# Delta-rule matmuls on unnormalised keys and queries, with the norms folded into row scalars

## The chip, the cores and the metric

The kernel runs on one core of a Trainium2 chip. The metric is the device time of one execution in microseconds (us). Engines are named as in the profile: PE is TensorE (matmuls; PEld its weight loads), DVE is VectorE, ACT is ScalarE, POOL is GpSimd, SP is the queue that issues the DMAs.

## The reference

One layer over x of shape (1, 1024, 1024) in float32: a mixer and a gated feed-forward block. The change concerns the mixer's head group A, a gated delta rule with 4 heads of 128 by 128. Its core, per head and per chunk of the sequence, is:

```
q, k = l2_normalize(q), l2_normalize(k)            # x * rsqrt(sum(x*x) + 1e-6), per token
L    = strict_lower((beta * k) @ k.T * decay)      # decay[i,j] = exp(gcum_i - gcum_j)
sol  = solve(I + L, [beta * v, beta * k * exp(gcum)])      # u, w
v_new = u - w @ state
o     = (q * exp(gcum)) @ state + lower(q @ k.T * decay) @ v_new
state = state * g_last + (k * exp(gcum_last - gcum)).T @ v_new
```

After it come a per-head RMS norm times a gate, an output projection together with head group B (attention in a sliding window), a residual, and the feed-forward block.

## The kernel before, in words

Three blocks follow each other: project_block (input projection and convolution; it leaves q, k, v per tile in DRAM with channels on the partitions), mix_block (both head groups, output projection, the residual and a norm), ffn_block. The change is in mix_block alone, in the profile about 281 to 713 us.

mix_block works on 8 tiles of 128 tokens. Every engine runs a list of small functions that is written out by hand: a preamble for tile 0, then step(t) for t = 0 to 7. In step t the functions named b_ advance the recurrence of tile t, those named a_ prepare head group A of tile t+1 (the flag a; absent in step 7), c_ are head group B of tile t+1, d_ the output projection of tile t-1 (flag d, from step 1) and the residual and norm of tile t-2 (flag e, from step 2). a_norms and a_square already belong to tile t+2 (flag n, absent from step 6 on). An engine does its list strictly in order; after(engine, counter, tile, k) makes it wait until a counter has reached its k-th event of that tile. PSUM banks have such counters too: full["a1"] counts the fills of a bank, free["a1"] the reads that release it, and fill(name, t, k) makes PE wait for the read k-1.

What matters here, in PE's order within a step: b_ks (keys times state), a_tr (k and v of the next tile to token order, in banks a0 and a1), b_vnew, a_sums (cumulated decays by column; it refills bank a1 and so waits for a_bv), d_tr, c_trq, b_o1 (queries times state), a_trk, b_ds (state update), c_trk, b_o2, a_kk, c_scores, a_kq, the output projection d_mm in pieces, a_trl, and then six levels of a_off and a_inv that build the inverse.

The norms before: a_square squares q and k of tile t+2 in the loaded block on ACT; a_norms sums over channels on PE with a column of ones; a_n2 adds 1e-6 on DVE; a_rnorm takes the power -0.5 on POOL, at the end of step t. a_khat on DVE then makes the unit keys k_tok from bank a0, a_trk and a_kt bring them to channel order in k_t, a_q copies the queries to q_t, a_kout on POOL scales k_tok to k_out, a_beta on POOL makes the mask beta * strict.

The loaded block qkv has one buffer, the left half of a stage; load_qkv waits until its readers are done.

## Time and profile before

| | |
|---|---|
| device time, median of 3 runs | 1465.1 us (1460.33 to 1465.41) |
| the profiled execution | 1462.3 us, of which the span is 1460.5 |
| instructions | 18291 |
| mix stage, first instruction to the first weights of ffn_block | 281 to 713 us |
| step 4 (b_ks of tile 4 to b_ks of tile 5) | 527.74 to 575.93, 48.2 us |
| mean granted clock of PE | 0.965 |

The span goes from the first to the last instruction. Times in the profile count from the start of the span. A granted clock of 1 is 2.4 GHz, of 0.5 is 1.2 GHz. Matmuls in float32 leave two records each, transposes and fp32r matmuls one. Records on PE overlap, so starts tell more than durations there.

### The profile page before, as it was taken

Reading aid. Unit: us, or ns where it says so; the run is one execution under the profiler, and the core shown is the slowest. Engines: PE = TensorE matmul, PEld = TensorE weight load, DVE = VectorE, ACT = ScalarE, POOL = GpSimd, SP = SyncE. Lnnn points to the kernel's source line nnn. Section 1 sums busy time; section 2 is a strip of 40 time slices with the busy share of each in tenths; the row PEclk is TensorE's granted clock in tenths of the full one; section 3 lists DMA queues with packets and bytes.
Section 4 is the critical chain, followed back from the end, with each engine's and each line's share of the span. In section 5 each row is a group of like instructions: output and inputs, shape, how many; then the busy total and the mean of one; then the engine's idle time right before and its main releaser. Section 6 shows DMA issues by size and latency. Waiting matters only on the chain.

```text
span 1460.5 us, 18291 instructions
## 1 busy us (share of the span) xinstructions
PE 1355.5 (93%) x6919; PEld 1145.0 (78%) x6919; DVE 720.7 (49%) x989; ACT 407.7 (28%) x672; POOL 198.9 (14%) x202
## 2 busy tenths in 40 slices
...
DMA packets 63707, 99.39 MB, mean 68 GB/s; under 512 B 4111, under 2 KB 48815, under 8 KB 63663
## 3 DMA queue, kind: packets, MB, share of 16 engines
...
## 4 chain that ended last, share of the span: by engine, by line
PE 48%; POOL 1%; DVE 1%; issue 1%; ACT 0%; POOLq 0%
PE f_ps_up L2038 11%; PE f_ps_up L2039 11%; PE f_ps_up L2040 11%; PE sums L2057 5%; PE sums L2058 5%; PE sums L2056 5%; POOL stage L1765 1%; POOL f_conv L1765 0%; DVE split L1963 0%; POOL f_stat L2022 0%; DVE f_w_lo L1904 0%; ACT f_w_hi L1836 0%; POOLq L1672 0%; DVE f_conv L1976 0%; DVE h_t L1956 0%
## 5 line engine op out<-in xcount | busy, mean ns | idle before, releaser
L2038 PE MATMUL f_ps_up<-split,f_w_hi 128*128 128x512 f32 x704 | 275.7, 392 | 2.2 <-DVE split L1963 2.2
L2039 PE MATMUL f_ps_up<-split,f_w_hi 128*128 128x512 f32 x704 | 275.3, 391 | 0.0
L2040 PE MATMUL f_ps_up<-split,f_w_lo 128*128 128x512 f32 x704 | 275.2, 391 | 0.0
L1909 DVE SCALAR_TENSOR_TENSOR f_conv<-f_ps_up,f_taps,f_conv 128x1023 f32<-128x1023 f32 x88 | 112.8, 1282 | 275.2 <-ACT f_conv L1840 269.7
L2038 PEld LDWEIGHTS f_ps_up<-split,f_w_hi 128*128 128x128 f32 x704 | 133.0, 189 | 30.8 <-DVE split L1963 2.0
L2040 PEld LDWEIGHTS f_ps_up<-split,f_w_lo 128*128 128x128 f32 x704 | 133.0, 189 | 27.8
L2039 PEld LDWEIGHTS f_ps_up<-split,f_w_hi 128*128 128x128 f32 x704 | 133.0, 189 | 27.5
L1840 ACT ACTIVATE f_conv<-f_ps_up,f_taps 128x1024 f32<-128x1024 f32 x44 | 53.2, 1209 | 325.9 <-PE f_ps_up L2040 325.9
L1921 DVE TENSOR_TENSOR h_t<-sums,h_t 128x512 f32<-128x512 f32 x176 | 116.3, 687 | 37.3 <-PE sums L2058 37.1
L2056 PE MATMUL sums<-f_w_hi,f_y_hi 128*128 128x512 f32 x320 | 124.5, 389 | 0.0
L2057 PE MATMUL sums<-f_w_lo,f_y_hi 128*128 128x512 f32 x320 | 124.5, 389 | 0.0
L2058 PE MATMUL sums<-f_w_hi,f_y_lo 128*128 128x512 f32 x320 | 124.5, 389 | 0.0
L2022 POOL TENSOR_TENSOR f_stat<-f_stat,f_power 128x1 f32<-128x1 f32 x8 | 5.4, 671 | 695.4 <-DVE f_stat L2006 695.4
L1904 DVE TENSOR_TENSOR f_w_lo<-stage,f_w_hi 128x2048 fp32r<-128x2048 f32 x33 | 75.6, 2290 | 49.0 <-ACT f_w_hi L1836 49.0
L474 PE MATMUL ps_g<-wbuf,tile_hi 128*128 128x512 f32 (+1 forms) x192 | 69.9, 364 | 6.4 <-DVE wbuf L409 6.4
L1429 PE MATMUL m_ps_a<-m_inv,m_low_t 128*128 128x128 f32 x384 | 57.5, 296 | 19.3 <-DVE m_inv L1148 17.0
L494 PE MATMUL ps_g<-h_hi,wbuf 128*128 128x512 f32 x192 | 74.8, 390 | 0.0
L496 PE MATMUL ps_g<-h_hi,wbuf 128*128 128x512 f32 x192 | 74.7, 389 | 0.0
L495 PE MATMUL ps_g<-h_lo,wbuf 128*128 128x512 f32 x192 | 74.7, 389 | 0.0
L1429 PEld LDWEIGHTS m_ps_a<-m_inv,m_low_t 128*128 128x128 f32 x384 | 50.7, 202 | 29.3 <-DVE m_inv L1148 25.4
L2056 PEld LDWEIGHTS sums<-f_w_hi,f_y_hi 128*128 128x128 f32 x320 | 60.1, 188 | 12.5
L2058 PEld LDWEIGHTS sums<-f_w_hi,f_y_lo 128*128 128x128 f32 x320 | 60.1, 188 | 12.5
...
## 6 DMA issues: line engine op xcount, KB each, us to landing
...
```

What stands on the lines that cost most here:

```text
L494: pe.matmul(bank, w_hi, h_hi[:, k, cols], start=(k == 0), stop=False)
L495: pe.matmul(bank, w_hi, h_lo[:, k, cols], start=False, stop=False)
L1429: op = pe.matmul(bank("a0")[:, h], low_t[:, h], inv[:, h], start=True, stop=True)
L1904: dve.tensor_tensor(w_lo[:, kind], raw[:, slot], w_hi[:, kind].bitcast(F32), ALU.subtract).then_inc(s_wlo, 1)
L1909: op = dve.scalar_tensor_tensor(conv[:, q, k:S], ps_up[:, q % 2, 0:S - k], taps[:, bass.ds(ct + (FTAPS - 1 - k) * 2 * FT, 1)], conv[:, q, ...
L1921: dve.tensor_tensor(cols, ps_dn[:, (2 * t + half) % 4], cols, ALU.add).then_inc(s_acc, 1)
L2038: pe.matmul(bank, hi, h_hi[:, k, cols], start=(k == 0), stop=False)
L2039: pe.matmul(bank, hi, h_lo[:, k, cols], start=False, stop=False)
L2040: op = pe.matmul(bank, lo, h_hi[:, k, cols], start=False, stop=(k == KD - 1))
L2056: pe.matmul(bank, y_of(0, last)[:, k, y], dn_w(0, kind)[:, k, cols], start=(k == 0), stop=False)
L2057: pe.matmul(bank, y_of(0, last)[:, k, y], dn_w(1, kind)[:, k, cols], start=False, stop=False)
L2058: op = pe.matmul(bank, y_of(1, last)[:, k, y], dn_w(0, kind)[:, k, cols], start=False, stop=(k == 1))
```

## The change

Keys and queries are no longer normalised before the matmuls. PE reads them straight from the loaded block, and the norms come in as one scalar per token and head:

- a_khat, a_trk, a_kt and a_q go, with k_tok, k_t and q_t. a_kk, a_kq, b_ks and b_o1 read qkv[par]. The block has two buffers, and load_qkv has other conditions.
- a_square and a_norms do the queries alone. The squares of the keys are summed by ACT (a_ksq) from bank a0, after a_tr of the same step and, in ACT's list, behind b_v_new. a_kn2 on DVE adds 1e-6.
- a_rnorm on POOL moves from the end of a step (for tile t+2) to the head of the next (for the same tile, then t+1). It makes the reciprocal key norm rn, then beta * rn, beta * rn * rn, and beta * rn * rn * I_NEG (I_NEG no longer holds beta), then the reciprocal query norm.
- a_bv scales by beta * rn; a_low takes beta * rn * rn by head in four instructions; b_resid takes the negative one. a_beta goes, and a_masks uses strict alone.
- a_kout moves from POOL to DVE, behind b_state, and reads bank a0; its read releases the bank for a_kk.

The diff, cut to its core (twelve leading blanks removed; the calls of the preamble, which follow the same order, and lines that only pass par on are left out):

```diff
@@ -578,12 +579,12 @@
 a_exp = sb("a_exp", [P, H])
 power = sb("power", [P, 2 * H])
-squares = sb("squares", [P, 2 * H, P])
+squares = sb("squares", [P, H, P])
+k_junk = sb("k_junk", [P, H, P], BF16)
 g_tri = sb("g_tri", [P, H, P])
 norm2 = sb("norm2", [P, 2, 2, 2 * H])
-k_tok = sb("k_tok", [P, H, P])
-k_t = sb("k_t", [P, H, P])
-q_t = sb("q_t", [P, H, P])
+k_gate = sb("k_gate", [P, 2, 3, H])
+K_RN, K_LOW, K_NEG = range(3)
 k_out = sb("k_out", [P, H, P])
 b_v = sb("b_v", [P, H, P])
 dec_t = sb("dec_t", [P, H, P])
@@ -712,10 +711,10 @@
         sp.wait_ge(s.sem, v)
         carry(sp)
-def load_qkv(u):
+def load_qkv(u, par):
     at = reg(u * (P * A_TILES * P))
-    ready((full["a1"], u - 1, 2), (qt_set, u - 1, 1), (squared, u - 1, 1))
-    sp.dma_start(flat(qkv), qkv_flat[bass.ds(at, P * A_TILES * P)].rearrange("(p n) -> p n", p=P)).then_inc(
+    ready((qkv_in, u - 1, 16), (full["b0"], u - 2, 1), (full["b1"], u - 2, 1))
+    sp.dma_start(flat(qkv[par]), qkv_flat[bass.ds(at, P * A_TILES * P)].rearrange("(p n) -> p n", p=P)).then_inc(
         qkv_in.sem, 16)
 def load_row(t):
@@ -810,23 +809,21 @@
     pool.tensor_tensor(g_tri[:], over_heads(tri), over_cols(gs[:, par, I_G]), ALU.mult).then_inc(tri_set.sem, 1)
 def a_rnorm(u, par):
-    after(pool, n2, u)
-    pool.tensor_tensor(norm2[:, par, 1], norm2[:, par, 0], power[:], ALU.pow).then_inc(rn.sem, 1)
-
-def a_kout(u, par):
-    after(pool, khat, u)
-    after(pool, full["b0"], u - 1, 3)
-    pool.tensor_tensor(k_out[:], k_tok[:], over_cols(gs[:, par, I_OUT]), ALU.mult).then_inc(kout_set.sem, 1)
-
-def a_beta(u, par):
+    after(pool, k_n2, u)
+    pool.tensor_tensor(norm2[:, par, 1, H:], norm2[:, par, 0, H:], power[:, 0:H], ALU.pow).then_inc(rn.sem, 1)
+    after(pool, rn, u, 1)
     after(pool, gs_set, u)
-    after(pool, n2, u)
-    pool.tensor_tensor(beta_low, over_heads(strict), over_cols(gs[:, par, I_BETA]), ALU.mult).then_inc(beta_set.sem, 1)
+    pool.tensor_tensor(k_gate[:, par, K_RN], norm2[:, par, 1, H:], gs[:, par, I_BETA], ALU.mult).then_inc(gate_set.sem, 1)
+    after(pool, gate_set, u, 1)
+    pool.tensor_tensor(k_gate[:, par, K_LOW], norm2[:, par, 1, H:], k_gate[:, par, K_RN], ALU.mult).then_inc(gate_set.sem, 1)
+    after(pool, gate_set, u, 2)
+    pool.tensor_tensor(k_gate[:, par, K_NEG], k_gate[:, par, K_LOW], gs[:, par, I_NEG], ALU.mult).then_inc(gate_set.sem, 1)
+    after(pool, q_n2, u)
+    pool.tensor_tensor(norm2[:, par, 1, 0:H], norm2[:, par, 0, 0:H], power[:, 0:H], ALU.pow).then_inc(rn.sem, 1)
 def a_masks(u):
     after(pool, dec_exp, u, 1)
-    after(pool, beta_set, u)
-    pool.tensor_tensor(dec[:], dec[:], beta_low, ALU.mult).then_inc(dec_masked.sem, 1)
+    pool.tensor_tensor(dec[:], dec[:], over_heads(strict), ALU.mult).then_inc(dec_masked.sem, 1)
     after(pool, dec_exp, u, 2)
     pool.tensor_tensor(dec_t[:], dec_t[:], over_heads(tri), ALU.mult).then_inc(dec_masked.sem, 1)
@@ -884,26 +881,22 @@
 pool.wait_ge(s_tab, 16)
 pool.wait_ge(s_gate, 1)
 a_gates(0, 0)
+c_kdup(0)
 a_rnorm(0, 0)
-a_beta(0, 0)
-c_kdup(0)
-a_kout(0, 0)
 c_kprev(0, 0)
 a_masks(0)
 pool.wait_ge(s_load, LOADS)
 a_init_t(0)
-a_rnorm(1, 1)
 a_gates(1, 1)
 b_zw(0)
 def step(t, par, n, a, d, e):
     if a:
-        a_beta(t + 1, 1 - par)
+        a_rnorm(t + 1, 1 - par)
     if e:
         d_rstd(t - 2, 1)
     if a:
         c_kdup(t + 1)
-        a_kout(t + 1, 1 - par)
         c_kprev(t + 1, 1 - par)
         a_masks(t + 1)
     b_scale(t, par)
@@ -916,7 +909,6 @@
     if a:
         b_zw(t + 1)
     if n:
-        a_rnorm(t + 2, par)
         a_gates(t + 2, par)
 steps(pool, step)
@@ -926,19 +918,17 @@
 @block.scalar
 def _(act):
-def a_square(u):
+def a_square(u, par):
     after(act, qkv_in, u)
-    after(act, dec_masked, u - 1, 1)
-    act.activation(squares[:], qkv[:, 0:2 * H], ACT.Square).then_inc(squared.sem, 1)
-
-def a_q(u):
-    after(act, full["b1"], u - 1, 1)
-    act.copy(q_t[:], qkv[:, 0:H]).then_inc(qt_set.sem, 1)
-
-def a_kt(u):
-    after(act, full["a0"], u, 2)
-    after(act, full["b0"], u - 1, 1)
-    act.copy(k_t[:], bank("a0")).then_inc(free["a0"].sem, 1)
+    after(act, full["a1"], u - 1, 1)
+    act.activation(squares[:], qkv[par][:, 0:H], ACT.Square).then_inc(squared.sem, 1)
+
+def a_ksq(u, par):
+    after(act, full["a0"], u, 1)
+    after(act, rn, u - 2, 1)
+    for h in range(H):
+        op = act.activation(k_junk[:, h], bank("a0")[:, h], ACT.Square, accum_out=norm2[:, par, 0, H + h:H + h + 1])
+    op.then_inc(k_sq.sem, 1)
 def a_exp_(u):
     after(act, clipped, u, 2)
@@ -1056,12 +1045,11 @@
         d_square(t - 2, 1)
     b_v_new(t)
     if a:
-        a_q(t + 1)
+        a_ksq(t + 1, 1 - par)
         c_qb(t + 1)
     if d:
         d_hi(t - 1)
     if a:
-        a_kt(t + 1)
         c_kb(t + 1, 1 - par)
         a_exp_(t + 1)
     b_square(t)
@@ -1096,20 +1084,24 @@
 def _(dve):
 def a_bv(u, par):
     after(dve, full["a1"], u, 2)
-    after(dve, gs_set, u)
+    after(dve, gate_set, u, 1)
     after(dve, free["b0"], u - 1, 1)
-    dve.tensor_tensor(b_v[:], bank("a1"), over_cols(gs[:, par, I_BETA]), ALU.mult).then_inc(free["a1"].sem, 1)
+    dve.tensor_tensor(b_v[:], bank("a1"), over_cols(k_gate[:, par, K_RN]), ALU.mult).then_inc(free["a1"].sem, 1)
 def a_n2(u, par):
     after(dve, full["a1"], u, 1)
     after(dve, o_rstd, u - 2)
-    dve.tensor_scalar(norm2[:, par, 0], ps["a1"][:, 0:2 * H], EPS, None, ALU.add).then_inc(n2.sem, 1)
-
-def a_khat(u, par):
-    after(dve, rn, u)
+    dve.tensor_scalar(norm2[:, par, 0, 0:H], ps["a1"][:, 0:H], EPS, None, ALU.add).then_inc(q_n2.sem, 1)
+
+def a_kn2(u, par):
+    after(dve, k_sq, u)
+    dve.tensor_scalar(norm2[:, par, 0, H:], norm2[:, par, 0, H:], EPS, None, ALU.add).then_inc(k_n2.sem, 1)
+
+def a_kout(u, par):
     after(dve, full["a0"], u, 1)
-    after(dve, kout_set, u - 1)
-    dve.tensor_tensor(k_tok[:], bank("a0"), over_cols(norm2[:, par, 1, H:2 * H]), ALU.mult).then_inc(khat.sem, 1)
+    after(dve, gs_set, u)
+    after(dve, full["b0"], u - 1, 3)
+    dve.tensor_tensor(k_out[:], bank("a0"), over_cols(gs[:, par, I_OUT]), ALU.mult).then_inc(free["a0"].sem, 1)
 def a_diff(u, par):
     after(dve, full["a1"], u, 3)
@@ -1119,10 +1111,13 @@
     after(dve, clipped, u, 1)
     dve.tensor_scalar(dec[:], dec[:], 0.0, None, ALU.max).then_inc(clipped.sem, 1)
-def a_low(u):
+def a_low(u, par):
     after(dve, dec_masked, u, 1)
-    after(dve, full["a0"], u, 3)
-    dve.tensor_tensor(low[:], bank("a0"), dec[:], ALU.mult).then_inc(free["a0"].sem, 1)
+    after(dve, gate_set, u, 2)
+    after(dve, full["a0"], u, 2)
+    for h in range(H):
+        op = dve.scalar_tensor_tensor(low[:, h], bank("a0")[:, h], k_gate[:, par, K_LOW, h:h + 1], dec[:, h], ALU.mult, ALU.mult)
+    op.then_inc(free["a0"].sem, 1)
 def a_qk(u):
     after(dve, dec_masked, u, 2)
@@ -1151,7 +1146,7 @@
 def b_resid(t, par):
     after(dve, full["b0"], t, 1)
     for h in range(H):
-        op = dve.scalar_tensor_tensor(resid[:, h], bank("b0")[:, h], gs[:, par, I_NEG, h:h + 1], b_v[:, h], ALU.mult, ALU.add)
+        op = dve.scalar_tensor_tensor(resid[:, h], bank("b0")[:, h], k_gate[:, par, K_NEG, h:h + 1], b_v[:, h], ALU.mult, ALU.add)
     op.then_inc(free["b0"].sem, 1)
 def b_state(t, par):
@@ -1294,23 +1290,25 @@
 def step(t, par, n, a, d, e):
     b_resid(t, par)
     if a:
-        a_bv(t + 1, 1 - par)
+        a_kn2(t + 1, 1 - par)
     if e:
         d_ms(t - 2, 1)
     if a:
-        a_khat(t + 1, 1 - par)
+        a_bv(t + 1, 1 - par)
     if e:
         d_res(t - 2)
     b_o1(t, par)
     if a:
         a_diff(t + 1, 1 - par)
     b_state(t, par)
+    if a:
+        a_kout(t + 1, 1 - par)
     if d:
         d_lo(t - 1)
     b_o(t)
     if a:
         c_max(t + 1, 0)
-        a_low(t + 1)
+        a_low(t + 1, 1 - par)
         a_qk(t + 1)
     b_ms(t)
     if a:
@@ -1369,23 +1367,22 @@
 def fill(name, t, k):
     after(pe, free[name], t if k > 1 else t - 1, k - 1 if k > 1 else None)
-def a_tr(u):
+def a_tr(u, par):
     after(pe, qkv_in, u)
     fill("a0", u, 1)
     for h in range(H):
-        op = pe.transpose(bank("a0")[:, h], qkv[:, H + h], ident)
+        op = pe.transpose(bank("a0")[:, h], qkv[par][:, H + h], ident)
     op.then_inc(full["a0"].sem, 1)
-    after(pe, n2, u)
+    after(pe, q_n2, u)
     for h in range(H):
-        op = pe.transpose(bank("a1")[:, h], qkv[:, 2 * H + h], ident)
+        op = pe.transpose(bank("a1")[:, h], qkv[par][:, 2 * H + h], ident)
     op.then_inc(full["a1"].sem, 1)
 def a_norms(u):
     after(pe, squared, u)
-    after(pe, qkv_in, u)
     fill("a1", u, 1)
-    for c in range(2 * H):
-        op = pe.matmul(ps["a1"][:, c:c + 1], squares[:, c], ones[:, 0:1], start=True, stop=True)
+    for h in range(H):
+        op = pe.matmul(ps["a1"][:, h:h + 1], squares[:, h], ones[:, 0:1], start=True, stop=True)
     op.then_inc(full["a1"].sem, 1)
 def a_sums(u):
@@ -1393,23 +1390,18 @@
     fill("a1", u, 2)
     pe.matmul(ps["a1"][:], ones, flat(g_tri[:]), start=True, stop=True).then_inc(full["a1"].sem, 1)
-def a_trk(u):
-    after(pe, khat, u)
+def a_kk(u, par):
+    after(pe, free["a0"], u, 1)
+    after(pe, k_sq, u)
     for h in range(H):
-        op = pe.transpose(bank("a0")[:, h], k_tok[:, h], ident)
+        op = pe.matmul(bank("a0")[:, h], qkv[par][:, H + h], qkv[par][:, H + h], start=True, stop=True)
     op.then_inc(full["a0"].sem, 1)
-def a_kk(u):
-    after(pe, free["a0"], u, 1)
+def a_kq(u, par):
+    fill("a2", u, 1)
+    after(pe, qkv_in, u)
     for h in range(H):
-        op = pe.matmul(bank("a0")[:, h], k_t[:, h], k_t[:, h], start=True, stop=True)
-    op.then_inc(full["a0"].sem, 1)
-
-def a_kq(u):
-    fill("a2", u, 1)
-    after(pe, qt_set, u)
-    for h in range(H):
-        op = pe.matmul(bank("a2")[:, h], k_t[:, h], q_t[:, h], start=True, stop=True)
+        op = pe.matmul(bank("a2")[:, h], qkv[par][:, H + h], qkv[par][:, h], start=True, stop=True)
     op.then_inc(full["a2"].sem, 1)
 def a_trl(u):
@@ -1601,20 +1592,19 @@
     A = (lambda f, *w: f(t + 1, *w)) if a else (lambda f, *w: None)
     D_ = (lambda f, *w: f(t - 1, *w)) if d else (lambda f, *w: None)
     after(pe, free["a2"], t)
-    b_ks(t)
-    A(a_tr)
+    b_ks(t, par)
+    A(a_tr, 1 - par)
     b_vnew(t)
     A(a_sums)
     D_(d_tr, 1 - par)
     A(c_trq)
-    b_o1(t)
-    A(a_trk)
+    b_o1(t, par)
     b_ds(t)
     A(c_trk)
     b_o2(t)
-    A(a_kk)
+    A(a_kk, 1 - par)
     A(c_scores, 1 - par, 0)
-    A(a_kq)
+    A(a_kq, 1 - par)
     D_(d_mm, 0, [0, 1, 2, 3])
     A(a_trl)
     D_(d_mm, 0, [4, 5, 6])
```

## Rows read from the trace of the kernel before

**Rows 1.** The page, part 1: engine, busy us (share of the span), count of instructions.

```profile
PE 1355.5 (93%) x6919; PEld 1145.0 (78%) x6919; DVE 720.7 (49%) x989; ACT 407.7 (28%) x672; POOL 198.9 (14%) x202
```

**Rows 2.** Stretches, step 4: stretch, us, then busy us of PE, PEld, DVE, ACT, POOL, clock, DMA.

```profile
527.74:575.93 48.19, 44.78 (x318) 39.61 (x318) 26.75 (x56) 17.53 (x50) 16.81 (x20) 0.98 0.16 55
```

**Rows 3.** Timeline, start of step 4: start us, us, engine, line, names, count.

```profile
530.93 0.69 DVE L1101 TENSOR_TENSOR m_b_v<-m_ps_a,m_gs 128x512 f32<-128x512 f32 x1
...
530.95 1.16 PE L1463 MATMUL sums<-m_resid,m_inv_t 128*128 128x128 f32 x8 [0.34 <-DVE m_resid L1154]
...
531.76 0.56 POOL L877 TENSOR_TENSOR m_d_stat<-m_d_stat,m_power 128x1 f32<-128x1 f32 x1 [2.86 <-DVE m_d_stat L1219]
...
531.95 1.02 PE L1394 MATMUL m_ps_a<-m_g_tri,m_table 128*128 128x512 f32 x2
...
532.23 0.59 ACT L959 COPY m_v_new<-sums 128x512 f32<-128x512 f32 x1 [4.67 <-PE sums L1463]
...
532.47 1.41 DVE L1227 SCALAR_TENSOR_TENSOR m_y<-sums,m_d_stat,g_post 128x512 f32<-128x512 f32 x2 [0.18 <-POOL m_d_stat L877]
...
533.27 0.66 PE L1532 MATMUL sums<-m_table,m_mix_a 128*128 128x128 f32 x4 [0.30 <-DVE m_y L1227]
...
534.86 1.06 PE L1469 MATMUL sums<-m_state,m_q_t 128*128 128x128 f32 x8
...
535.75 0.60 PE L1399 MATMUL m_ps_a<-m_table,m_k_tok 128*128 128x128 f32 x4
...
536.19 1.06 PE L1476 MATMUL sums<-m_v_new,m_k_out 128*128 128x128 f32 x8
...
538.57 1.16 PE L1405 MATMUL m_ps_a<-m_k_t 128*128 128x128 f32 x8
...
544.13 0.60 PE L1419 MATMUL m_ps_a<-m_table,m_low 128*128 128x128 f32 x4
```

**Rows 4.** Timeline, the same stretch, VectorE (DVE) and GpSimd (POOL).

```profile
535.95 0.69 DVE L1166 TENSOR_TENSOR stage<-sums,m_gs 128x512 f32<-128x512 f32 x1 [2.08 <-PE sums L1469]
...
537.33 1.27 POOL L819 TENSOR_TENSOR m_k_out<-m_k_tok,m_gs 128x512 f32<-128x512 f32 x1 [4.66 <-PE sums L1476]
...
538.80 1.11 DVE L1161 SCALAR_TENSOR_TENSOR m_state<-m_state,m_gs,sums 128x128 f32<-128x128 f32 x4
```

**Rows 5.** Instructions of tiles m_o_stat and m_dec: ns min/median/max.

```profile
L870 POOL TENSOR_TENSOR m_o_stat<-m_o_stat,m_power x8: 1015/1382/1385, 350.9 to 681.9; 128x4 f32<-128x4 f32 x8
...
L873 POOL TENSOR_TENSOR m_o_stat<-m_o_stat,m_norm x8: 198/200/203, 352.3 to 683.0; 128x4 f32<-128x4 f32 x8
...
L1120 DVE TENSOR_SCALAR m_dec<-m_dec x8: 427/1145/1145, 299.6 to 633.8; 128x512 f32<-128x512 f32 x8
```

**Rows 6.** Timeline, ScalarE (ACT), b_square of step 4, first and last record.

```profile
541.75 0.31 ACT L965 ACTIVATE m_junk_o<-stage 128x128 bf16<-128x128 f32 x1 [1.42 <-DVE stage L1171]
...
542.85 0.19 ACT L965 ACTIVATION_READ_ACCUMULATOR m_junk_o<-stage 128x1 f32 x1
```

**Rows 7.** Timeline, TensorE, end of step 4: the squares' column sums.

```profile
571.71 1.84 PE L1388 MATMUL m_ps_a<-m_table,m_squares 128*128 128x1 f32 x16
```

**Rows 8.** Stretches: from the last a_off to b_resid in three steps; an idle stretch and after.

```profile
521.10:529.80 8.70, 8.70 (x57) 8.29 (x55) 1.98 (x7) 1.71 (x3) 3.83 (x4) 0.80 0.00 1
...
470.90:480.40 9.50, 9.50 (x55) 8.94 (x54) 1.98 (x7) 1.70 (x3) 3.83 (x4) 0.71 0.01 2
...
570.10:577.10 7.00, 7.00 (x56) 6.59 (x55) 1.95 (x7) 1.71 (x3) 3.10 (x4) 1.00 0.00 0
...
692.90:695.90 3.00, 0.04 (x1) 0.02 (x1) 1.04 (x3) 1.12 (x2) 0.55 (x1) 1.00 0.00 0
...
696.00:704.00 8.00, 6.50 (x21) 4.86 (x22) 3.25 (x5) 2.33 (x4) 2.90 (x2) 0.57 0.24 83
```

**Rows 9.** Timeline, TensorE, step 0: c_trq and its wait.

```profile
341.54 0.66 PE L1489 MATMUL m_ps_c<-m_table,stage 128*128 128x128 f32 x4 [1.65 <-DMA stage<-rows]
```

**Rows 10.** Timeline, TensorE, step 4: the longest standstill in its middle.

```profile
552.08 1.16 PE L1429 MATMUL m_ps_a<-m_inv,m_low_t 128*128 128x128 f32 x8 [1.56 <-DVE m_inv L1148]
```

More of the change, by code:

```diff
@@ L567, in mix_block @@
         left, right = stage[:, 0], stage[:, 1]
-        qkv = left[:, 0:A_TILES * P].rearrange("p (c s) -> p c s", s=P)
+        late = sb("qkv_odd", [P, A_TILES * P])
+        qkv = [m.rearrange("p (c s) -> p c s", s=P) for m in (left[:, 0:A_TILES * P], late[:])]
         zw = left[:, A_TILES * P:(A_TILES + H) * P].rearrange("p (h c) -> p h c", c=P)
@@ L596, in mix_block @@
         off = sb("off", [P, H, P])
-        beta_low = squares[:, 0:H]
         state = sb("state", [P, H, P])
@@ L647, in mix_block @@
         gs_set, tri_set, squared = tally("gs_set"), tally("tri_set"), tally("squared")
-        n2, rn, khat, qt_set, kout_set = (tally(n) for n in ("n2", "rn", "khat", "qt_set", "kout_set"))
+        q_n2, k_n2, k_sq, rn, gate_set = tally("q_n2"), tally("k_n2"), tally("k_sq"), tally("rn", 2), tally("gate_set", 3)
         clipped, dec_exp, dec_masked = tally("clipped", 2), tally("dec_exp", 2), tally("dec_masked", 2)
-        beta_set, init, init_t = tally("beta_set"), tally("init", 2), tally("init_t", 2)
+        init, init_t = tally("init", 2), tally("init_t", 2)
         st_set, o1_set, o_set = tally("st_set"), tally("o1_set"), tally("o_set")
@@ L765, in _ @@
             sp.dma_start(h_t[:], w_rows).then_inc(s_w, 16)
-            load_qkv(1)
+            load_qkv(1, 1)
             def step(t, par, n, a, d, e):
@@ L772, in step @@
                 if n:
-                    load_qkv(t + 2)
+                    load_qkv(t + 2, par)
                 if e:
@@ L782, in _ @@
             last = T - 1
-            ready((full["a1"], last, 2), (qt_set, last, 1), (squared, last, 1), (full["c0"], last, 1), (kdup_set, last, 1),
+            ready((full["a1"], last, 2), (full["b0"], last, 1), (full["b1"], last, 1), (squared, last, 1), (full["c0"], last, 1), (kdup_set, last, 1),
                   (zw_set, last, 1), (o_sq, last, 1), (mixa, last, 1))
@@ L861, in b_scale @@
                 rq = norm2[:, par, 1, 0:H]
-                after(pool, rn, t)
+                after(pool, rn, t, 2)
                 pool.tensor_tensor(o_stat[:, 1], rq, rq, ALU.mult).then_inc(o_n.sem, 1)
@@ L1032, in _ @@
             act.activation(gates[:, :, I_OUT], g_tmp[:, 4], ACT.Exp).then_inc(s_ga, 1)
-            a_square(0)
-            a_q(0)
+            a_square(0, 0)
+            a_ksq(0, 0)
             c_qb(0)
-            a_kt(0)
             c_kb(0, 0)
@@ L1043, in _ @@
             a_invt(0, 2)
-            a_square(1)
+            a_square(1, 1)
             a_invt(0, 3)
@@ L1077, in step @@
                 if n:
-                    a_square(t + 2)
+                    a_square(t + 2, par)
                 if a:
@@ L1139, in a_off @@
             def a_off(u, n):
-                after(dve, full["a0"], u, 3 + n)
+                after(dve, full["a0"], u, 2 + n)
                 if n == 1:
```

28 lines of the change are left out of this document (14 added, 14 removed).

## The prediction

> **What bounds the kernel now.** I read the page first. TensorE is busy for 93% of the span [rows 1], so it looks like the bound everywhere; but the change touches only the mix stage, which lasts from 281 to about 704 us, and the chain that ended last begins after it. So I went to the stretches. From one b_ks to the next, 527.74 to 575.93, a step takes 48.2 us, of which TensorE shows 44.8 us busy [rows 2]: its queue is nearly full, and it is worked off strictly in the order written down. There are eight steps, t = 0 to 7, and seven of them (0 to 6) carry the A work of the next tile. In such a queue two things count: the time in which TensorE issues, and whether the head of the queue can go when its turn comes. The timeline of step 4 shows both. b_vnew starts at 530.95, and a_sums follows at 531.95 without a wait, because a_bv, which frees its bank, had run on VectorE from 530.93 to 531.62 [rows 3]. Then come d_tr (533.27), c_trq, b_o1 (534.86), a_trk (535.75), b_ds (536.19), a_kk (538.57), and a_trl at 544.13 [rows 3]. The reader is to see that a_sums today depends on nothing that b_vnew produces.
>
> **What the change takes from TensorE.** a_trk goes: four transposes, 536.19 - 535.75 = 0.44 us of issue [rows 3]. a_norms falls from 16 records to 8: half of 1.84, about 0.9 us [rows 7]; it stands among work whose inputs are ready, so I count it in full (0.85). That is 1.3 us a step at most. The three other matmul groups read the loaded block where they read k_t and q_t, at the same shapes: no change.
>
> **What it adds: the gate chain.** a_bv no longer multiplies by a beta that has long been ready, but by beta times the key norm, and that norm is begun only in this step. In order: ScalarE must first do b_v_new, which waits for b_vnew: it runs from 532.23 to 532.82 [rows 3]. Only behind it stands a_ksq. Four squares with a sum each took 541.75 to 543.04, 1.29 us, in b_square [rows 6]: done at 534.1. a_kn2 is a tiny VectorE operation; with its two handovers I put it at 0.3 us, an estimate between nothing and the 0.69 us of a full 512-column one [rows 3]: 534.4. Then GpSimd: a power over four columns took 1.015 to 1.385 us [rows 5]. I take 1.02, the short end, since VectorE stands still meanwhile, and the two engines can slow each other (the max operation of [rows 5] took 0.427 us alone and 1.145 beside GpSimd); the other end costs 0.36 more. 535.5. The first product, 0.20 us by its like [rows 5], gives 535.8 with the handover. a_bv: 0.15 us handover (as from 532.32 to 532.47) and 0.69 [rows 3], so 536.65. a_sums therefore starts near 536.65 and not at 531.95: **4.7 us late**, with TensorE standing at the head of its queue, and everything of the step behind it. On VectorE the waiting a_kn2 and a_bv hold back d_res and b_o1; on ScalarE c_qb and d_hi stand behind a_ksq, and both have inputs that are later still.
>
> **The second delay, through GpSimd.** a_rnorm now stands ahead of d_rstd(t-2, 1) in GpSimd's queue. After the first product come two more (about 0.3 us each), then the power for the queries (1.02 to 1.38), then d_rstd, which ran for 0.56 us at 531.76 before [rows 3]. That ends near 538.15. VectorE's d_res waits for it and starts at 538.3 where it started at 532.47 [rows 3]: 5.8 us late. d_tr needs the banks that d_res frees, so the whole queue from d_tr on (c_trq, b_o1) is 5.8 us late. This part is absent in steps 0 and 1, which have no d_res.
>
> **The third, through a_kout.** Before, a_kk waited for the copy to k_t, and came 538.57 - 534.86 = 3.71 us after b_o1. Now it waits for a_kout on VectorE, behind b_state. VectorE's part of b_o1 starts 535.95 - 534.86 = 1.09 after TensorE's; from there to b_state it is 538.80 - 535.95 = 2.85 us [rows 3, 4]. In this stretch the max operation took 1.145 us, its median; its shortest was 0.427 [rows 5]. GpSimd's k_out, which ran beside it from 537.33 to 538.60 [rows 4], goes, so I let 0.72 come off: 2.13. Then b_state 1.11, a_kout 0.69 (priced as a_bv, same shape), 0.05 handover: 1.09 + 2.13 + 1.11 + 0.69 + 0.05 = 5.07. a_kk is another 5.07 - 3.71 = **1.4 us late**. The 0.44 of a_trk lies in this same stretch, which VectorE now closes: it is worth nothing. a_kk and a_trl stand 5.56 us apart, filled by TensorE itself [rows 3]. a_low in four pieces is 0.42 longer (1.11, as b_state, against 0.69), and a_kout and the d_lo behind it push it back, but it ends about 4.3 us behind a_kk and is hidden by those 5.56.
>
> **The rest.** GpSimd loses a_beta and k_out (1.27 us [rows 4]), ScalarE two copies and half a square: all beside the path. The load of block t+2 keeps its place in SP's queue behind load_row and load_v; it waits for b_ks and b_o1 of step t instead of the copies of tile t+1, and is out some 6 us after its old time. Its first reader, a_square, stands late in the step's list, behind the second a_invt: hidden. Without that cover up to these 6 us would come on top of a step. The preamble has the gate chain once, but half of a cold a_norms less and no b_v_new ahead: nothing, by 1 us either way.
>
> **The sum.** Steps 2 to 5: 5.8 + 1.4 - 0.85 = 6.35, four times, 25.4. Step 6 has no a_norms: 7.2. Step 1: 4.7 + 1.4 - 0.85 = 5.25. Step 0 already waited 1.65 us for a transfer ahead of c_trq [rows 9], which the delay swallows: 3.6. Together **41.5 us**.
>
> **The clock.** Before, the granted clock fell to 1.2 GHz for a few microseconds around b_ks in most steps. The same stretch of a step, up to b_resid, took 8.7 us with such a dip (0.80), 9.5 with a long one (0.71), and 7.0 with none [rows 8]: 1.6 to 2.5 us each. And after 3.0 us in which TensorE did nothing (692.9 to 695.9) the clock stood at 0.57 over the 8 us that follow [rows 8]. The new standstill is longer, and two shorter ones follow it in the same 12 us, so I expect a dip in every step, 1.6 to 2.5 us, while some of the old ones go with the one-column records of a_norms. Bounds: from -1.6 a step (no new dip, old ones gone) to +6.6 or so (below). I take +1.3 for each of seven, 9 us, nearest to a single dip in each step less some old ones. The Trainium skill (TensorE: Matmul & The Clock Gate, "The HAM clock gate") has the half rate as the default, lifted only by sustained activity. By that the lower level would last for as long as the step's start is broken by waits, and the sum would be that of the long dip below.
>
> The profiled execution took 1462.3 us for a span of 1460.5, 2.8 under the median of the three runs (1465.1) and inside them. 1462.3 + 41.5 + 9 = **1513 us**, 3.3% above the median. Less than 0.5% (7 us) could not be told from no change.
>
> **Rivals.**
> Chain without clock: the waits cost as summed, but no new dips, and the old ones go: 1496 to 1504. For it: one standstill of 1.56 us [rows 10] brought no dip in its step. Against: 3.0 us were followed by one.
> Long dip: the clock stays low from a_sums to a_trl. From a_sums to a_trl TensorE took 12.2 us before; without the 2.8 from a_trk to a_kk, which VectorE now covers, and about 1 us of waits, some 8.3 us of work lie on the path. A stretch of 8.7 us at 0.80 holds 3.5 us at the lower level and cost 1.7, so each microsecond of work costs up to one more, 6.6 to 8.3 a step: 1550 or more. Against it: the last 5.56 us are dense.
> TensorE's issue is all that counts (the other side): the gate comes in time because the waits of a step that exist now take the delay up. Then only the 1.3 us a step stay: 7 x 1.3 = 9 off, 1453. It decides if the chain behind b_vnew is under 1 us; and a step has only 3.4 us without TensorE work in all [rows 2], while ScalarE's four squares alone need 1.3.
> Half hidden: GpSimd's powers or a_ksq take half of what I put: near 1485.
> No change: gain and delay cancel, which needs a delay of 1.3 us a step.
>
> **How the numbers follow.** Forecast (chain and short dips, 1500 to 1530) 0.58; chain without clock 0.17; long dip 0.12; half hidden 0.05; TensorE alone 0.05; no change 0.03. The range 1492 to 1534 holds the first two and the near tail of the third and leaves out about 0.2; the slower ends of powers (+0.7 a step, 5 us) lie in it. Slower 0.92, same 0.03, faster 0.05.
>
> **What would show it.** Right: a_sums 5 to 6 us behind b_vnew, released by b_v on VectorE; VectorE waiting for GpSimd at a_bv, GpSimd for a_kn2; d_res about 1.7 us after a_bv; a_kk released by a_kout; steps of 54 to 57 us, the last as before; a granted clock under 1 in the first third of each step. Wrong: a_sums within 2 us of b_vnew, steps under 50 us, or stretches outside 281 to 704 that change.

## The result and the profile after

The changed kernel takes 1504.2 us (median of 4 runs, 1504.0 to 1504.46) against 1465.3 (4 runs, 1460.33 to 1468.4): 1.028 times the time, 95% interval 1.026 to 1.031. It is slower by 39 us; 1513 was forecast, with a range of 1492 to 1534. The profiled execution took 1504.0 us for a span of 1502.2.

The page of the changed kernel, part 1, to be read against [rows 1]:

```profile
PE 1356.7 (90%) x6823; PEld 1140.8 (76%) x6823; DVE 719.7 (48%) x1021; ACT 404.7 (27%) x720; POOL 189.0 (13%) x218
```

TensorE has 96 records fewer and yet the same busy time: what it lost in work it spends at the lower clock, and the mean granted clock went from 0.965 to 0.955. The 41.7 us between the two profiled executions are standstill, and they lie in the mix stage. b_ks of tile 0 starts 2.6 us later than before (337.06 against 334.50), seven steps follow that are 40.1 us longer together (375.73 against 335.62), and what comes after is 1.0 us shorter.

Step 4, timeline of all engines, in the columns of [rows 3]:

```profile
552.42 1.16 PE L1455 MATMUL sums<-m_resid,m_inv_t 128*128 128x128 f32 x8 [0.35 <-DVE m_resid L1149]
553.70 0.59 ACT L949 COPY m_v_new<-sums 128x512 f32<-128x512 f32 x1 [3.07 <-PE sums L1455]
554.18 0.28 ACT L930 ACTIVATE m_k_junk<-m_ps_a 128x128 bf16<-128x128 f32 x1
...
555.10 0.23 ACT L930 ACTIVATION_READ_ACCUMULATOR m_k_junk<-m_ps_a 128x1 f32 x1
555.36 0.17 DVE L1098 TENSOR_SCALAR m_norm<-m_norm 128x4 f32<-128x4 f32 x1 [3.00 <-ACT m_k_junk L930]
...
555.61 1.01 POOL L813 TENSOR_TENSOR m_norm<-m_norm,m_power 128x4 f32<-128x4 f32 x1 [21.29 <-DVE m_norm L1098]
556.70 0.20 POOL L816 TENSOR_TENSOR m_k_gate<-m_norm,m_gs 128x4 f32<-128x4 f32 x1
...
557.04 0.69 DVE L1089 TENSOR_TENSOR m_b_v<-m_ps_a,m_k_gate 128x512 f32<-128x512 f32 x1 [1.40 <-POOL m_k_gate L816]
...
557.79 2.08 PE L1391 MATMUL m_ps_a<-m_g_tri,m_table 128*128 128x512 f32 x2 [4.21 <-DVE m_b_v L1089]
558.39 0.56 POOL L874 TENSOR_TENSOR m_d_stat<-m_d_stat,m_power 128x1 f32<-128x1 f32 x1
...
559.10 1.41 DVE L1222 SCALAR_TENSOR_TENSOR m_y<-sums,m_d_stat,g_post 128x512 f32<-128x512 f32 x2 [1.36 <-POOL m_d_stat L874]
...
559.90 1.12 PE L1524 MATMUL sums<-m_table,m_mix_a 128*128 128x128 f32 x4
...
561.66 1.06 PE L1481 MATMUL m_ps_c<-m_table,stage 128*128 128x128 f32 x4
...
562.52 1.86 PE L1461 MATMUL sums<-m_state,stage 128*128 128x128 f32 x8
...
566.20 0.43 DVE L1112 TENSOR_SCALAR m_dec<-m_dec 128x512 f32<-128x512 f32 x1
...
566.54 1.12 DVE L1156 SCALAR_TENSOR_TENSOR m_state<-m_state,m_gs,sums 128x128 f32<-128x128 f32 x4
...
567.57 0.69 DVE L1104 TENSOR_TENSOR m_k_out<-m_ps_a,m_gs 128x512 f32<-128x512 f32 x1
...
568.31 1.16 PE L1397 MATMUL m_ps_a<-m_qkv_odd 128*128 128x128 f32 x8 [1.94 <-DVE m_k_out L1104]
...
571.50 1.12 DVE L1119 SCALAR_TENSOR_TENSOR m_low<-m_ps_a,m_k_gate,m_dec 128x128 f32<-128x128 f32 x4
...
573.90 0.60 PE L1411 MATMUL m_ps_a<-m_table,m_low 128*128 128x128 f32 x4
```

Read it down the brackets. a_sums (557.79) comes 5.37 us behind b_vnew where it came 1.00 behind, and TensorE stands still for 4.21 us until b_v is written. VectorE had waited for the gate, GpSimd for a_kn2, VectorE for ScalarE's squares. That is the forecast chain link by link. Then a_sums takes 2.08 us where it took 1.02 in [rows 3]. Behind it four transposes of d_tr take 1.12 us, where they took 0.66, and the four of c_trq 1.06 us, 0.66 in [rows 9]. And a_kk (568.31) waits for k_out on VectorE.

The stretches of the same step, in the columns of [rows 2] (the last three figures are clock, DMA share, GB/s):

```profile
550.09:605.89 55.80, 47.03 (x306) 41.17 (x306) 26.64 (x60) 17.84 (x58) 16.27 (x21) 0.91 0.14 47
546.30:553.30 7.00, 6.65 (x53) 6.19 (x52) 2.39 (x9) 1.11 (x2) 0.00 (x0) 1.00 0.01 2
...
558.00:564.00 6.00, 5.96 (x21) 4.39 (x22) 1.41 (x2) 1.24 (x3) 1.30 (x3) 0.50 0.00 0
564.00:566.00 2.00, 2.00 (x20) 2.00 (x19) 1.55 (x3) 0.79 (x3) 0.00 (x0) 0.95 0.36 46
```

The granted clock is at its lower level, 1.2 GHz, for all of 558 to 564. It falls before the standstill is over, here at 557.4, and does so in every one of the seven steps, for 6.8 us in six of them and for 3.4 in step 1. Around b_ks, where it had been low in most steps ([rows 8], 0.80 and 0.71), it is now at 1.00. So a low stretch came and another one went.

**Where it went, over seven steps.** The table adds up, for steps 0 to 6, the time from one start in TensorE's timeline to the next (a_off: the last one, on VectorE). The last column is the sum of a row; the starts are rounded, so a figure can be 0.1 off. It holds the experiments too; which kernel each is stands below.

| kernel | b_ks to b_vnew | to a_sums | to c_trq | to b_o1 | to a_kk | to a_trl | to last a_off | to b_ks | sum |
|---|---|---|---|---|---|---|---|---|---|
| before | 21.2 | 7.7 | 16.9 | 3.1 | 25.8 | 37.9 | 180.8 | 42.3 | 335.6 |
| after | 16.3 | 38.2 | 24.5 | 5.6 | 38.0 | 39.4 | 181.0 | 32.7 | 375.7 |
| e5, squares twice | 16.3 | 45.3 | 24.7 | 5.3 | 36.0 | 39.4 | 180.2 | 32.7 | 379.9 |
| e2, d_rstd first | 16.3 | 38.2 | 22.5 | 4.7 | 36.8 | 42.7 | 182.3 | 32.7 | 376.2 |
| e4, filler | 16.3 | 38.2 | 18.9 | 3.1 | 35.0 | 45.7 | 183.3 | 32.7 | 373.1 |
| e10, both | 16.3 | 38.1 | 11.9 | 3.0 | 35.0 | 42.3 | 179.7 | 32.7 | 359.0 |
| e3, a_kout first | 17.5 | 37.6 | 24.7 | 5.8 | 30.5 | 37.8 | 189.5 | 32.7 | 376.0 |
| e1, norms as before | 21.0 | 7.2 | 11.4 | 3.1 | 34.9 | 42.7 | 181.1 | 41.1 | 342.4 |
| e6, before, half the norms | 16.3 | 7.0 | 16.9 | 3.1 | 25.7 | 37.9 | 185.4 | 32.7 | 325.0 |
| e8, late scale | 17.7 | 7.3 | 14.9 | 3.1 | 35.7 | 39.1 | 184.7 | 32.7 | 335.1 |
| e9, late scale, early a_kout | 16.5 | 7.0 | 14.9 | 3.0 | 30.3 | 38.7 | 180.7 | 32.7 | 323.8 |

### The profile page after: what moved, and what is told of

Its sections match the earlier page's. It is cut to its first block and busy times, and to the rows that moved or that the text cites. A ratio compares the mean times of both kernels' runs of the same rounds, so it can differ in the third digit from the quotient of the medians.

```text
span 1502.2 us, 18183 instructions
## 1 busy us (share of the span) xinstructions
PE 1356.7 (90%) x6823; PEld 1140.8 (76%) x6823; DVE 719.7 (48%) x1021; ACT 404.7 (27%) x720; POOL 189.0 (13%) x218
## 5 line engine op out<-in xcount | busy, mean ns | idle before, releaser
L1421 PEld LDWEIGHTS m_ps_a<-m_inv,m_low_t 128*128 128x128 f32 x384 | 52.3, 208 | 28.3 <-DVE m_inv L1143 24.5
L2047 PEld LDWEIGHTS sums<-f_w_lo,f_y_hi 128*128 128x128 f32 x320 | 60.1, 188 | 12.5
```

The lines of the kernel that those rows point to most:

```text
L1421: op = pe.matmul(bank("a0")[:, h], low_t[:, h], inv[:, h], start=True, stop=True)
L2047: pe.matmul(bank, y_of(0, last)[:, k, y], dn_w(1, kind)[:, k, cols], start=False, stop=False)
```

## The experiments

Ratios are against runs of the kernel before on the same chip. All edits but e6's are to the changed kernel, and are shown cut to their core.

**Is the gate's chain the path, with slope one?** e5 makes it longer.

```diff
 def a_ksq(u, par):
     after(act, full["a0"], u, 1)
     after(act, rn, u - 2, 1)
+    for h in range(H):
+        act.activation(junk2[:, h], bank("a0")[:, h], ACT.Square, accum_out=extra[:, h:h + 1])
     for h in range(H):
```

> The changed kernel, with a_ksq's four squares done twice (same tiles, the second time over the first), so that the gate's chain behind b_vnew is about 1.15 us longer in each step; the results are the same. If the chain b_vnew, squares, power, gate, a_bv, a_sums sets the end of every step with slope one, the time goes up by 1.05 to 1.15 us x 7 (+1 for the preamble): 1511 to 1514 against 1504 of the changed kernel, with +-3 for stretches of low clock that move. If the chain had slack (rival: the 4.4 us ahead of a_sums is the low clock's and not the chain's), 1504 stays.

1511.4 us, ratio 1.034 (1.031 to 1.037): 7.2 us above the changed kernel. Timeline of its step 4: the first new square, the last old one, a_sums.

```profile
559.75 0.28 ACT L932 ACTIVATE m_junk<-m_ps_a 128x128 bf16<-128x128 f32 x1
...
561.66 0.26 ACT L934 ACTIVATION_READ_ACCUMULATOR m_k_junk<-m_ps_a 128x1 f32 x1
...
564.38 2.07 PE L1395 MATMUL m_ps_a<-m_g_tri,m_table 128*128 128x512 f32 x2 [5.24 <-DVE m_b_v L1093]
```

a_sums stands 1.02 us further behind b_vnew in each of the seven steps, 7.1 together, and the preamble is 1.4 longer: up to a_sums there is no slack in the chain. The rest moves too: the steps win 3.0 us back behind a_sums, mostly between b_o1 and a_kk and in the middle of step 4, and 2.5 come on top behind the steps, where the clock is low for 6.8 us more than in the changed kernel.

**Taken out by computing the norms early.** e1 goes back to the path of before for the key norms: squares of q and k on ScalarE from the block, 16 column sums in a_norms for tile t+2, one power over eight columns at the end of a step. The gate factors, raw keys and a_kout stay as changed.

```diff
 # POOL, end of step, in place of its head
     if n:
         a_gates(t + 2, par)
+        a_rnorm(t + 2, par)
 # PE, a_norms
-    for h in range(H):
+    for h in range(2 * H):
```

> The changed kernel (1504.2 us), with the key norms made as before the change: ScalarE squares queries and keys, TensorE sums both with its column of ones (16 records again), and GpSimd makes the norms and the three key scalars at the end of the step before. a_ksq and a_kn2 are gone; all else of the change stays (raw keys and queries, two blocks, a_kout on VectorE behind b_state, a_low in four pieces). Gate theory: a_sums follows b_vnew within 1.3 us again, d_res starts as early as before the change, and of the step's delay only that of a_kout stays: 7 x (4.4 + 1.3) = 40 off less 6 x 0.87 = 5 for the longer a_norms and some 5 for dips of the clock around b_ks that come back: 1474, range 1468 to 1482. Rival, a_kout and the longer a_low: the wait for the gate is only where VectorE's lateness shows first, and nearly all of the 39 us stays: above 1490.

1477.7 us (10 runs), ratio 1.010 (1.007 to 1.013), inside the expected range. From b_vnew to a_sums it is 7.2 again. In the steps, what stays is mainly the way from b_o1 to a_kk, 34.9 against 25.8, which is a_kout's. Another 5.6 us lie ahead of them: b_ks of tile 0 starts at 340.12, at 334.50 in the kernel before. With the 16 column sums the low clock around b_ks is back too: 21.0 and 41.1, near the 21.2 and 42.3 of before.

**The second delay alone.** e2 puts d_rstd ahead of a_rnorm on GpSimd, and d_ms ahead of a_kn2 on VectorE.

```diff
 # POOL, step
-    if a:
-        a_rnorm(t + 1, 1 - par)
     if e:
         d_rstd(t - 2, 1)
     if a:
+        a_rnorm(t + 1, 1 - par)
         c_kdup(t + 1)
```

> The changed kernel with two pairs swapped: on GpSimd d_rstd of tile t-2 stands ahead of a_rnorm, on VectorE d_ms ahead of a_kn2. Gate theory: d_res then follows a_bv directly instead of 1.36 us later (557.73 against 559.10 in step 4), TensorE's d_tr follows a_sums by 1.0 instead of 2.1 us; five steps have it (2 to 6): 5 x 1.1 = 5.5 off: 1498.7, range 1496 to 1502. Rival, a_kout: d_res is hidden by the VectorE work behind it, no change: 1504.

1505.8 us, ratio 1.027 (1.021 to 1.034): nothing gained where 5.5 were expected, a miss. Timeline of step 3 (d_res, a_sums, d_tr), and a stretch behind its a_kk:

```profile
503.26 1.40 DVE L1222 SCALAR_TENSOR_TENSOR m_y<-sums,m_d_stat,g_post 128x512 f32<-128x512 f32 x2
...
503.40 2.08 PE L1391 MATMUL m_ps_a<-m_g_tri,m_table 128*128 128x512 f32 x2 [4.02 <-DVE m_b_v L1089]
...
505.26 1.06 PE L1524 MATMUL sums<-m_table,m_mix_a 128*128 128x128 f32 x4
```

```profile
514.00:516.00 2.00, 2.00 (x11) 2.00 (x11) 0.95 (x3) 1.13 (x8) 0.20 (x1) 0.50 0.00 0
```

d_res now runs directly behind a_bv, as meant; but d_tr has to wait for a_sums anyway, which at the lower clock takes 2.08 us. The slow a_sums covers the late d_rstd. Only 2.8 us are won up to b_o1 and 1.2 from there to a_kk, and 4.6 come back where the clock is low now (0.50 here; "to a_trl" 42.7 against 39.4, and 1.3 behind it).

**The low clock alone.** e4 keeps TensorE at work while it waits for a_bv: four unused 128x512 matmuls (eight records) into a free bank.

```diff
     b_vnew(t)
+    if a:
+        for _ in range(4):
+            pe.matmul(ps["a2"][:], ident, table[:, 0:HALF], start=True, stop=True)
     A(a_sums)
```

> The changed kernel with four more matmuls a step (identity by 512 columns of the table, float32, into the idle bank a2) between b_vnew and a_sums; their result is read by nobody. They fill about 3.5 to 4 of the 4.2 us in which TensorE stands still. Clock theory: the clock stays at 2.4 GHz through the start of the step; against the same stretches of the profile at the lower level (sm to trq 0.4, c_trq 0.42, to a_kk 0.5, and 1.2 for a dip in the middle of step 4) that gives 1.3 us a step, 9 off: 1495, range 1492 to 1499. Rival: the lower clock hides behind waits for the other engines, and the time stays within 3 us of 1504, or rises if the filler outlasts the wait.

1503.1 us, ratio 1.026 (1.020 to 1.033): 1.1 us gained where 9 were expected, a miss. Timeline of its step 4: filler, a_sums, d_res, d_tr; then two later stretches of the step.

```profile
548.74 3.60 PE L1600 MATMUL m_ps_a<-m_table 128*128 128x512 f32 x8
...
553.12 1.12 PE L1391 MATMUL m_ps_a<-m_g_tri,m_table 128*128 128x512 f32 x2 [0.78 <-DVE m_b_v L1089]
...
554.42 1.41 DVE L1222 SCALAR_TENSOR_TENSOR m_y<-sums,m_d_stat,g_post 128x512 f32<-128x512 f32 x2 [1.36 <-POOL m_d_stat L874]
...
555.23 0.66 PE L1524 MATMUL sums<-m_table,m_mix_a 128*128 128x128 f32 x4 [0.99 <-DVE m_y L1222]
```

```profile
560.00:562.00 2.00, 0.19 (x1) 0.19 (x2) 2.00 (x7) 1.15 (x2) 1.52 (x2) 1.00 0.79 329
...
564.00:566.00 2.00, 2.00 (x11) 2.00 (x11) 1.48 (x5) 0.86 (x6) 0.20 (x1) 0.50 0.00 0
```

a_sums is quick again, 1.12 us, and now d_tr waits 0.99 us for d_res. 11.2 us are won from a_sums to a_kk. But the clock falls later instead, behind the wait for k_out (560 to 562), which in the changed kernel brought no dip in this step. There TensorE fills the time by itself: a_kk to a_trl takes 7.2 us in four steps where it took 5.6, and 5.7 in step 0 where it took 4.3. In step 1 it is the other way round, 5.6 where it took 7.2. With what comes on top in the middle of the steps, 8.6 us come back in all.

**Both together.** e10 has the edits of e2 and of e4.

> The changed kernel with the two edits that alone gave nothing, together: the eight unused matmuls on TensorE while it waits for a_bv, and d_rstd ahead of the key norms' power on GpSimd. Theory (each hid the other: the slow a_sums covered the late d_rstd, and the late d_rstd covered the quick a_sums): from the end of a_bv to c_trq 0.8 us less in 5 steps, 0.3 to 0.4 less up to b_o1 and some 0.5 less up to a_kk, together about 8 us, 1496, if no stretch of low clock appears elsewhere. Rival (a stretch of low clock moves into the later, TensorE-bound part of the step, as in the run with the filler alone): 1.2 to 1.6 us more there in 4 to 5 steps, 1501 to 1504.

1487.4 us, ratio 1.018 (1.015 to 1.020): 17 us faster than the changed kernel, where the edits alone moved it by -1.1 and +1.6. My figure of 1496 was too high, and the rival's 1501 to 1504 is out. Timeline of its step 4:

```profile
550.85 1.40 DVE L1222 SCALAR_TENSOR_TENSOR m_y<-sums,m_d_stat,g_post 128x512 f32<-128x512 f32 x2
...
550.98 1.13 PE L1391 MATMUL m_ps_a<-m_g_tri,m_table 128*128 128x512 f32 x2 [0.78 <-DVE m_b_v L1089]
...
551.95 0.60 PE L1524 MATMUL sums<-m_table,m_mix_a 128*128 128x128 f32 x4
...
553.25 1.06 PE L1461 MATMUL sums<-m_state,stage 128*128 128x128 f32 x8
```

From a_sums to b_o1 it is 2.27 us, against 4.73 in the changed kernel, and d_tr waits for nothing. Neither edit could give this alone, since each wait lay beside the other. Behind a_kk the clock is low in the first three steps only (0, 1 and 2), where e4 has it in five, so less comes back.

**The third delay alone.** e3 puts a_kout ahead of b_state on VectorE.

```diff
-    b_state(t, par)
     if a:
         a_kout(t + 1, 1 - par)
+    b_state(t, par)
```

> The changed kernel with a_kout ahead of b_state on VectorE. Gate theory with its third delay: a_kk starts earlier by the length of b_state, 1.12 us, in seven steps: 7.8 off, 1496.4, range 1494 to 1500, if a_low doesn't become the limit in place of a_kk. Rival, only the gate counts: a_kk is hidden by what follows, 1504.

1505.3 us, ratio 1.027 (1.021 to 1.033): missed. The edit does what it should, 30.5 to a_kk in place of 38.0, and 1.6 to a_trl. But 8.5 us come back in the middle of the steps. From the timeline of its step 3, and the stretch from 526 on:

```profile
525.85 2.07 PE L1421 MATMUL m_ps_a<-m_inv,m_low_t 128*128 128x128 f32 x8 [1.34 <-DVE m_inv L1143]
```

```profile
526.00:528.00 2.00, 2.00 (x10) 2.00 (x11) 0.04 (x1) 0.00 (x0) 0.00 (x0) 0.50 0.54 217
```

The clock falls behind a wait in the inverse's levels, and eight records take 2.07 us where 1.16 is usual [rows 10]. So it is in six of its steps, and in one (step 4) of the changed kernel.

**Were the old dips tied to the column sums?** e6 is the kernel before without the key norms: a_norms sums the queries alone, 8 records of one column, and the query norms stand in for those of the keys.

```diff
 def a_norms(u):
-    for c in range(2 * H):
+    for c in range(H):
         op = pe.matmul(ps["a1"][:, c:c + 1], squares[:, c], ones[:, 0:1], start=True, stop=True)
```

> The kernel before with one part of the change alone: a_norms sums the queries' squares only, 8 records of one column in place of 16 (the keys are then scaled with the queries' norms, so the key norms are left out of the computation; GpSimd's power has four columns). The step's work term: 0.87 us off in six steps, 5 us, 1459. If the dips of the clock around b_ks (1.6 to 2.5 us, in most steps of before) come from the one-column records, they go too: 8 to 10 us more, 1450. Rival from the first four runs, a dip only changes its place when work is taken away: 1459 or more, with dips elsewhere in the step.

1451.6 us (10 runs) against 1460.2, ratio 0.995 (0.993 to 0.997). Timeline of its step 4, a_norms, to be read against [rows 7]; then the stretch around it, up to b_vnew of step 5.

```profile
559.85 0.95 PE L1388 MATMUL m_ps_a<-m_table,m_squares 128*128 128x1 f32 x8
```

```profile
556.37:565.50 9.13, 8.79 (x68) 8.01 (x65) 3.31 (x11) 2.29 (x4) 3.21 (x4) 1.00 0.00 0
```

The work saved is 0.90 us in each of six steps, 5.4: from the last a_off to b_ks step 4, in which the clock had stayed up there, goes from 5.86 to 4.96 us. But 14.5 us go around b_ks ("to b_ks" 32.7, "to b_vnew" 16.3). The other 9.1 are the clock's, which no longer falls there in any step; 4.6 come back in the middle. The table says the same of every kernel: with 16 column sums (before, e1) the two columns are 42 or 41 and 21, with 8 they are 32.7 and 16 to 18 (the 18 from step 0 alone).

**Using the wait.** e7 gives TensorE other work ahead of a_sums: c_trq, b_o1 and a_kq.

```diff
     b_vnew(t)
-    A(a_sums)
-    D_(d_tr, 1 - par)
     A(c_trq)
     b_o1(t, par)
+    A(a_kq, 1 - par)
+    A(a_sums)
+    D_(d_tr, 1 - par)
     b_ds(t)
```

> The changed kernel with TensorE's list reordered: c_trq, b_o1 and a_kq, which need nothing of the gate, stand between b_vnew and a_sums. Gate theory: a_sums comes as late as before (VectorE's a_bv releases it), but 2.2 us of work are then done in the wait, and VectorE's b_o1 and all behind it start right after d_res: a_kk some 3.7 us earlier in a step, a_trl 4.6. 5 x 4.6 and 2 x 3 for steps 0 and 1: 29 off, 1475. As in the first runs the clock may give back 1.2 to 1.6 in half of the steps: 1480, range 1474 to 1487. Rival, VectorE's a_kout and a_low bind: above 1495.

1484.0 us, ratio 1.019 (1.015 to 1.022): inside the expected range. Timeline of its step 4:

```profile
542.91 1.06 PE L1404 MATMUL m_ps_a<-m_qkv_odd 128*128 128x128 f32 x8
545.95 1.12 PE L1391 MATMUL m_ps_a<-m_g_tri,m_table 128*128 128x512 f32 x2 [1.99 <-DVE m_b_v L1089]
```

a_sums stands as far behind b_vnew as before this edit (5.36 us), but only 1.99 of it is idle, and a_sums runs at full clock.

**Taking a_bv off the chain.** In e8, a_bv copies the values unscaled as soon as they are there; the factor beta * rn comes later, by one GpSimd product on b_v (a_vscale, at the end of the step), ahead of b_resid, its only reader. d_rstd stands first on GpSimd, and on VectorE a_bv comes right behind b_resid and a_kn2 behind d_res. e9 is e8 with a_kout ahead of b_o1 on VectorE, and two buffers for k_out, so that it needn't wait for b_ds.

```diff
+def a_vscale(u, par):
+    after(pool, free["a1"], u, 1)
+    pool.tensor_tensor(b_v[:], b_v[:], over_cols(k_gate[:, par, K_RN]), ALU.mult).then_inc(bv_set.sem, 1)
 def a_bv(u, par):
-    after(dve, gate_set, u, 1)
-    dve.tensor_tensor(b_v[:], bank("a1"), over_cols(k_gate[:, par, K_RN]), ALU.mult).then_inc(free["a1"].sem, 1)
+    dve.tensor_copy(b_v[:], bank("a1")).then_inc(free["a1"].sem, 1)
```

> The changed kernel with the wait for the gate removed in another way than by early norms: a_bv copies v out of the bank unscaled, and GpSimd scales it in place at the end of the step (1.3 us more on GpSimd); a_kn2 stands behind d_res, a_rnorm behind d_rstd. The keys' norms are still made late, by ScalarE, and a_norms keeps its 8 records. Gate theory: as with the early norms (1477.7), less 6 x 0.87 for a_norms: 1472, range 1465 to 1479. Rival, the late ScalarE squares and GpSimd powers disturb by themselves: near 1504.

> The one before it, with k_out in two buffers, so that a_kout stands ahead of b_o1 on VectorE, where that engine waits. Theory of the third delay: a_kk no longer waits, comes about 3.0 us behind b_o1 instead of 5.0, and seven steps lose 2.0 each: 14 off that one, 1458, range 1453 to 1466 with what the clock gives back; at or below the kernel before (1464). Rival, a_low (four pieces, 0.43 longer) takes over from a_kout: no more than 5 us better than that one.

e8: 1460.7 us (10 runs), ratio 1.001 (0.999 to 1.004), which is 11 below my figure and outside its range. That figure was worked out from e1; in e8 the clock is low around b_ks in step 0 alone, and the preamble is 4.3 us shorter than in e1 (b_ks of tile 0 at 335.78 against 340.12). e9: **1449.8 us** (10 runs), ratio 0.995 (0.992 to 0.997), 8 below my figure, also outside its range, and faster than both kernels, though than the kernel before by half a percent only. Its step 4, timeline (a_bv, a_sums, a_kout, a_kk) and the whole step:

```profile
522.20 0.69 DVE L1094 COPY m_b_v<-m_ps_a 128x512 f32<-128x512 f32 x1
...
523.22 1.02 PE L1396 MATMUL m_ps_a<-m_g_tri,m_table 128*128 128x512 f32 x2
...
525.45 0.69 DVE L1109 TENSOR_TENSOR m_k_out<-m_ps_a,m_gs 128x512 f32<-128x512 f32 x1
...
529.88 1.06 PE L1402 MATMUL m_ps_a<-m_qkv_odd 128*128 128x128 f32 x8
```

```profile
519.89:566.21 46.32, 42.47 (x306) 37.32 (x306) 27.00 (x60) 17.75 (x58) 17.22 (x22) 1.00 0.16 57
```

a_sums and a_kk wait for nothing, and the step is at full clock from end to end: 46.3 us, with the same 306 TensorE records that took 55.8 in the changed kernel.

## Why the prediction held, and where it was off

The mechanism was right: three waits, in the places named, released by the tiles named. Its sizes, against what the runs showed, in us over seven steps:

| step of the prediction | forecast | measured | from |
|---|---|---|---|
| a_sums late (4.7 x 7) | 32.9 | 30.5 | after, "to a_sums" |
| d_rstd (1.1 x 5), less 1.65 in step 0 | 3.9 | 1.9 | e4, "to c_trq" and "to b_o1", at full clock |
| a_kk late (1.4 x 7) | 9.8 | 9.2 | e4 and e10, "to a_kk", at full clock |
| a_norms (0.85 x 6) | -5.1 | -5.4 | e6 against before, steps without a dip: 0.90 each |
| new low clock | part of 9 | +12.9 | after less e4, the same columns (11.2), and +1.7 behind a_kk |
| old low clock gone | part of 9 | -9.1 | after less before, first and last column (-14.5), less the 5.4 |
| sum (of unrounded rows) | 50.5 | 40.1 | |

With 2.6 us in the preamble, for which I had put nothing, and -1.0 behind the steps this is the 41.7 us of the two profiled executions. The seven steps took 52.3 to 55.8 us, and only two of them the 54 to 57 that I had named as a sign.

**The gate's chain** was 4.1 to 4.4 us late in six steps (5.1 in step 0), not 4.7: the four squares took 1.15 us and began 0.11 us ahead of the end of b_v_new, where I had them end to end and at 1.29. The choice of the short end for the power was right: 1.01 us. By e5 the chain counts with slope one up to a_sums, so the rival in which the step's waits take it up is out. The half-hidden one is out by the two durations, 1.15 and 1.01 us, which are not half of what I put.

**The second delay** exists (d_res 1.36 us behind a_bv, released by d_rstd), but I had it too large. At full clock (e4, steps 2 to 6) it brings 0.7 us a step from a_sums to c_trq, not 1.1: d_res starts 6.68 us behind b_vnew against 1.52 in [rows 3], 5.2 late and not 5.8. In the changed kernel nearly all of it lies beside an a_sums at the lower clock, so that taking it out alone gave nothing (e2). e10, in which d_tr waits for nothing, where it waited 0.30 even before the change [rows 3], is 1.4 us a step quicker there than e4.

**The third** was right, also in its parts: the max operation fell to 0.43 us with k_out gone from GpSimd, and a_kk comes 4.99 us behind b_o1 at full clock (5.07 forecast). The Trainium skill (SBUF — State Buffer, "SBUF: two separate sides") says that VectorE, in some of its operations, and GpSimd share a port pair, which whichever starts first holds for its whole instruction. The trace agrees: in the kernel before, the max operation took 1.145 us in all seven steps, beside k_out, and 0.427 in the preamble, where it began behind k_out's end; in the changed kernel it is 0.43 everywhere.

**The clock** is the term that was most off: 9 us forecast, 3.8 measured. The new dips are there, 12.9 us or 1.8 a step, within the 1.6 to 2.5 I gave them. What failed is that only "some of the old ones go": all of them went, 9.1 us, and e6 shows that halving the column sums does this by itself, in the kernel before as well. So the size came out at the upper edge of the rival "chain without clock" (1496 to 1504), though its mechanism, no new dips, is refuted by the clock of 0.50 from 558 to 564. The long dip did not come: from 564 to 566 the clock was 0.95 again. The Trainium skill (TensorE: Matmul & The Clock Gate, "The HAM clock gate") has the lower rate last until activity is sustained; read as I read it for that rival, the wait ahead of a_kk (1.94 us, at 568.31) should have kept it low, and the trace disagrees.

**Open.** What decides where the clock falls once the waits move was not settled. e2, e3 and e4 each won 4 to 11 us where they should, and lost 5 to 9 to low stretches elsewhere in the step, while e7, e9 and e10 kept their gain. I can show that this happened in each, not foretell in which kernel it will. In e9's step 0 alone a_kk comes 7.5 us behind b_o1, not 3.7, since c_trk waits 3.33 us for c_kdup's copy on GpSimd; no run tried to take this away.
